# Weight low halves of the middle block by a negated copy and an adding transfer, the S5 recurrence on one engine, and a last section by token tiles

## What is computed

```
u = rms_norm(x, norm_pre);  p = u @ ev_w_in            # 1024 x 5120
a_in, a_z, b_val, b_gate, b_z = split(p)
ya = s5_layer(a_in, ...)        # s_t = Lbar s_{t-1} + Bbar u_t, 64 groups x 64 complex states
ya = gelu(ya); ya = ya * sigmoid(ya @ s5_w_glu + b_glu); ya = ya * silu(a_z)
h = b_val * sigmoid(b_gate)
h = causal depthwise conv of width 31 over the tokens
yb = (silu(layer_norm(h)) @ w_pw + b_pw) * silu(b_z)
x = x + rms_norm(concat([ya, yb]) @ ev_w_out, norm_post)
```

## Time and profile before

| | us |
|---|---|
| median of 3 runs (lowest, highest) | 1820.9 (1819.47, 1821.16) |
| the profiled execution, device time | 1818.73 |
| its span | 1817.0 |
| TensorE busy in the span | 1680.5 (92%) |
| VectorE busy | 1005.8 (55%) |
| ScalarE busy | 610.4 (34%) |
| GpSimd busy | 296.3 (16%) |
| mean granted TensorE clock, of full speed | 0.969 |

### The profile page before, as it was taken

The page is one execution under the profiler, slowest core; times in us unless marked ns, Lnnn a source line. Parts: engine busy times, 40 slices in busy tenths (PEclk is TensorE's granted clock), DMA queues, the critical chain, the costliest instruction groups (busy, mean ns, idle before and its releaser), DMA issues.

```text
span 1817.0 us, 20356 instructions
## 1 busy us (share of the span) xinstructions
PE 1680.5 (92%) x7876; PEld 1364.0 (75%) x7876; DVE 1005.8 (55%) x1271; ACT 610.4 (34%) x852; POOL 296.3 (16%) x316
## 2 busy tenths in 40 slices
PE   6999989999999999989977876999989999999995
PEld 5887878878888888879955656768877777787764
DVE  4375254552345244547999979965454344354434
ACT  4333322233212233343411214255245244243431
POOL 4980000000000000030199284200000000000000
PEclk9999999999999999999988898999999999999998
DMA  8556433233333322263312231115313122131211
GB/s 243 131 146 161 118 103 94 93 116 109 100 93 98 100 93 99 76 232 93 117 35 58 70 139 47 47 64 170 105 47 93 59 82 92 46 105 57 70 47 58
DMA packets 129467, 177.39 MB, mean 98 GB/s; under 512 B 50683, under 2 KB 61419, under 8 KB 128363
## 3 DMA queue, kind: packets, MB, share of 16 engines
q1 hardware_dynamic: 127563, 173.62, 30.9%
q10 hardware_dynamic: 1664, 2.13, 0.4%
q0 software_dynamic: 160, 0.52, 0.2%
HBM read 161.58 MB, written 14.68 MB: 97 GB/s over the span
## 4 chain that ended last, share of the span: by engine, by line
PE 76%; DVE 19%; ACT 2%; issue 1%; POOL 1%; SPq 0%; DMA 0%; ACTq 0%; DVEq 0%; POOLq 0%
PE PS L1960 67%; DVE TMP L1639 8%; DVE WL L1295 2%; PE PS L1938 2%; PE PS L2210 1%; PE PS L2228 1%; DVE FIX L1676 1%; DVE S L1678 1%; PE PS L2081 1%; PE PS L2219 1%; ACT XN L901 1%; DVE V L1373 1%; DVE SEGV L1610 1%; DVE S L1621 1%; DVE S L1618 1%
## 5 line engine op out<-in xcount | busy, mean ns | idle before, releaser
L1960 PE MATMUL PS<-HH,WH 128*128 128x512 f32 x1216 | 485.4, 399 | 46.5 <-DVE WL L1295 35.5
L1295 DVE TENSOR_TENSOR WL<-WR,WH 128x1024 fp32r<-128x1024 f32 x200 | 256.3, 1289 | 466.3 <-ACT WH L896 466.2
L1960 PE MATMUL PS<-HL,WH 128*128 128x512 f32 x1216 | 479.8, 395 | 0.0
L1960 PE MATMUL PS<-HH,WL 128*128 128x512 f32 x1216 | 479.3, 394 | 0.0
L896 ACT ACTIVATE WH<-WR 128x1024 fp32r<-128x1024 f32 x200 | 210.7, 1059 | 709.1 <-PE PS L1960 695.7
L1960 PEld LDWEIGHTS PS<-HH,WH 128*128 128x128 f32 x1216 | 232.6, 191 | 103.0 <-DVE WL L1295 30.7
L1960 PEld LDWEIGHTS PS<-HL,WH 128*128 128x128 f32 x1216 | 232.9, 192 | 49.1 <-issue 1.0
L1960 PEld LDWEIGHTS PS<-HH,WL 128*128 128x128 f32 x1216 | 232.3, 191 | 49.6
L1639 DVE SCALAR_TENSOR_TENSOR TMP<-CP,PRM,TMP 128x512 f32<-128x512 f32 x232 | 183.7, 838 | 0.0
L1960 PE MATMUL PS<-WH,HH 128*128 128x512 f32 x384 | 152.6, 397 | 6.5 <-DVE WL L1295 4.2
L1960 PE MATMUL PS<-WH,HL 128*128 128x512 f32 x384 | 151.6, 395 | 0.0
(11 more groups left out here) (312 smaller groups left out, 2039.3 us busy)
## 6 DMA issues: line engine op xcount, KB each, us to landing
WR<-in_w_in_dram SPq DMA_DIRECT2D x96, 512.0 KB, 3.7
WR<-in_ev_w_in_dram SPq DMA_DIRECT2D x40, 512.0 KB, 3.6
WR<-in_od_w_in_dram SPq DMA_DIRECT2D x32, 512.0 KB, 3.9
WR<-in_ev_w_out_dram SPq DMA_DIRECT2D x16, 512.0 KB, 3.6
WR<-in_od_w_in_dram SPq DMA_DIRECT2D x32, 256.0 KB, 3.3
WR<-in_od_w_out_dram SPq DMA_DIRECT2D x16, 512.0 KB, 3.8
WR<-in_w_branch_a_dram SPq DMA_DIRECT2D x8, 512.0 KB, 3.6
WR<-in_w_branch_b_dram SPq DMA_DIRECT2D x8, 512.0 KB, 3.6
```

The source lines that it names most:

```text
L1295: dve.tensor_tensor(WL[:, s, :, :], WR[:, s, :, :], WH[:, s, :, :].bitcast(F32), ALU.subtract).then_inc(w_lo, 1)
L1960: mm = pe.matmul(out_banks[m], st, mv, start=(kt == 0 and i == 0), stop=(kt == 2 * per - 1 and i == 2))
```

## The change

1. **Low halves.** For the chunks from a_in.0 to pw.1 (14 units, 56 chunks) VectorE no longer subtracts. ScalarE makes WH as before and right behind it WL = -W (L873 of the new kernel, semaphore w_neg). GpSimd then issues a transfer for each chunk that reads W from DRAM again and adds it onto WL in SBUF, whose landing counts w_summed of the slot; TensorE waits for w_summed instead of w_lo. As written, the low half comes out as the weight, rounded and negated, plus the weight. SP loads a chunk when w_neg says that the one four before is negated.
2. **Recurrence.** All 32 pairs on VectorE: 15 steps of five instructions of 512, 512, 512, 256 and 256 elements per partition, 7 carries of five short instructions, and 64 corrections of 420 elements. Fourteen steps and two instructions stand ahead of the gating of b_gate.1. GpSimd has none of it and does not gate YA either; VectorE does that.
3. **Order of taps.** 78 taps before the recurrence, 36 after it, 8 in the halves of y, 16 and 21 around glu, and the last 89 after everything that VectorE does for glu.
4. **Order of jobs.** TensorE runs glu, ev_a.0, mean, ev_a.1, var, pw. The centring reads the mean from PSUM.
5. **Last head.** Each token tile has both column halves made before the next; VectorE adds and weighs each half as it comes, ScalarE squares it; after a tile's second half one root, one reciprocal and one full-width operation follow.

```diff
@@ semaphores of the ring
+        w_neg, w_summed = sem("w_neg"), [sem(f"w_summed{i}") for i in range(RING)]
@@ SP
-                if n >= RING:
+                if summed(n - RING):
+                    sp.wait_ge(w_neg, n - RING - SUM_FROM + 1)
+                elif n >= RING:
                     sp.wait_ge(w_lo, n - RING + 1)
@@ GpSimd
+            def add_weights(job):
+                name, u = job.split(".")
+                for q in range(4):
+                    n = chunks_before(job) + q
+                    pool.wait_ge(w_neg, n - SUM_FROM + 1)
+                    pool.dma_start(WL[:, n % RING, :, :],
+                                   summands[name][q * 2 * P:(q + 1) * 2 * P, int(u) * NC:int(u) * NC + NC]
+                                   .rearrange("(k p) n -> p k n", p=P), accum_op=ALU.add).then_inc(w_summed[n % RING], 16)
@@ ScalarE
                     act.activation(WH[:, n % RING, :, :], WR[:, n % RING, :, :], ACT.Copy).then_inc(w_hi, 1)
+                    if summed(n):
+                        act.activation(WL[:, n % RING, :, :], WR[:, n % RING, :, :], ACT.Copy, scale=-1.0).then_inc(w_neg, 1)
...
             ya_halves(range(4, 8))
 
+            split()
+            act.wait_ge(h_lo, 32)
+            evac("ev_a.0", [YO[:, m, 0:NC] for m in range(4)], ACT.Copy)
             for kt in range(KT):
                 act.wait_ge(z_cent, kt + 1)
                 act.activation(SQ[:, kt, :], CP[:, kt, CPAD:], ACT.Square).then_inc(z_sq, 1)
             split()
-            act.wait_ge(h_lo, 32)
-            evac("ev_a.0", [YO[:, m, 0:NC] for m in range(4)], ACT.Copy)
+            evac("ev_a.1", [YO[:, m, NC:D] for m in range(4)], ACT.Copy)
             act.wait_ge(sq_used, KT)
             act.activation(RS[:, :], bank("var", 0), ACT.Sqrt, bias=EPS[:, 0:1]).then_inc(banks_act, 1)
@@ VectorE
-            split_convolve(24)
-            split_convolve(24)
-            convolve(44)
-            steps = step_ops()
-            split_convolve(20, steps)
-            split_convolve(12, steps)
+            convolve(78)
+            s5 = recurrence()
+            recur(s5, 42.0)
             times_tmp([("b_gate.1", m, CP[:, 4 + m, CPAD:]) for m in range(4)], GATEV)
             dve.wait_ge(tmp_free, 24)
-            split_convolve(20, steps)
-            split_convolve(24, steps)
-            for _ in steps:
+            for _ in s5:
                 pass
...
+            convolve(36)
...
                     convolve(1)
+                    dve.tensor_tensor(YA[:, kt, :], YA[:, kt, :], AZ[:, kt, :], ALU.mult).then_inc(ya_gated, 1)
...
-            split_convolve(24)
-            convolve(len(todo))
+            convolve(16)
             for u in range(2):
                 if u:
-                    split()
+                    convolve(21)
                     h_low(3, lambda kt: YA[:, kt, :], range(4))
                 dve.wait_ge(ya_gated, 4 * u + 4)
                 times_tmp([(f"glu.{u}", m, YA[:, 4 * u + m, :]) for m in range(4)], GLUV)
             h_low(3, lambda kt: YA[:, kt, :], range(4, 8))
+            convolve(len(todo))
@@ VectorE, the end
+            for t in range(TT):
+                last_add(t, 0)
+                if t == 0:
+                    dve.wait_ge(prow1_in, 16)
+                weigh(t, 0)
+                last_add(t, 1)
+                weigh(t, 1)
+                last_norm(t)
@@ TensorE
             section("glu", Y, ready(y_lo, 3))
+            section("ev_a", H, ready(h_lo, 3), rows=True, units=(0,))
             pe.wait_ge(ones_in, 1)
             pe.wait_ge(conv_done, 8)
...
-            section("ev_a", H, ready(h_lo, 3), rows=True, units=(0,))
+            section("ev_a", H, ready(h_lo, 3), rows=True, units=(1,))
             free("var")
...
-            section("ev_a", H, ready(h_lo, 3), rows=True, units=(1,))
             section("pw", Y, ready(y_lo, 4))
@@ TensorE, the last head
+                for t in range(1, TT):
+                    for u in range(2):
+                        for kt in range(4):
+                            step(t, u, kt)
```

More of the change, by code:

```diff
@@ L824, in _ @@
[L824 to L844, removed]
-                    tt(fix, by, end, ALU.mult)
-                    seq.wait()
-                    o = pool.tensor_tensor(into, into, fix, op)
-                    if q and n in (FIX_HALF - 1, len(FIX_POOL) - 1):
-                        o.then_inc(fixed_pool, 1)
-                        pool.wait_ge(fixed_pool, 1 + (n > FIX_HALF))
-                    else:
-                        seq.inc(o)
@@ L854, in _ @@
-            pool.wait_ge(banks_act, act_after("a_z2.1"))
-            for kt in range(KT):
-                pool.wait_ge(y_lo, 24 + kt + 1)
-                pool.tensor_tensor(YA[:, kt, :], YA[:, kt, :], AZ[:, kt, :], ALU.mult).then_inc(ya_gated, 1)
+            pool.tensor_scalar(LAM64[:, 2, :].unsqueeze(2), TAB[:, 1, :, SEG_CH - 1:SEG_CH], -1.0, None,
+                               ALU.mult, ALU.bypass).then_inc(powers, 1)
+            ev_in, ev_out = a["ev_w_in_2"][0], a["ev_w_out_2"][0]
+            summands = {"a_in": ev_in[:, EV_IN["a_in"]:], "b_val": ev_in[:, EV_IN["b_val"]:], "b_gate": ev_in[:, EV_IN["b_gate"]:],
+                        "a_z2": ev_in[:, EV_IN["a_z2"]:], "b_z2": ev_in[:, EV_IN["b_z2"]:], "glu": a["s5_w_glu_2"][0],
+                        "ev_a": ev_out[0:D, :], "pw": a["conv_w_pw_2"][0]}
@@ new lines, in recurrence @@
+                seq.wait(last)
+                dve.memset(BNA[:, 0, 0:1], 0.0).then_inc(carried, 1)
+                used = [last, last]
+                for b in range(FIX_BLOCKS):
+                    for q in range(2):
+                        made = []
+                        for ri in range(2):
+                            fix, into, by, end, op = correction(b, ri, q, ri)
+                            seq.wait(used[ri])
+                            made.append(seq.inc(dve.tensor_tensor(fix, by, end, ALU.mult)))
+                            yield 0.59
+                        for ri in range(2):
+                            fix, into, by, end, op = correction(b, ri, q, ri)
+                            seq.wait(made[ri])
+                            used[ri] = seq.inc(dve.tensor_tensor(into, into, fix, op))
+                            yield 0.59
+                    if b % 4 == 3:
+                        seq.wait(used[1])
+                        dve.memset(BNA[:, 0, 0:1], 0.0).then_inc(fixed, 1)
@@ L1880, in head @@
                 dve.wait_ge(y2_add, h * 8 + 8)
-                for u in range(2):
-                    if u and not last:
+                for u in range(0 if last else 2):
+                    if u:
                         hsplit(n, HEAD_CHUNKS + V_AT, 2)
@@ L2172, in _, with out_by_tile, step @@
             pe.wait_ge(banks_act, act_after("lr"))
+            def out_by_tile(n0, acts, kt_ready):
+                def step(t, u, kt):
+                    for i, (wi, ai) in enumerate(halves):
+                        mm = pe.matmul((B, A)[u][t], tile(acts(kt)[ai], t), (WH, WL)[wi][:, 2 * u + kt // 2, kt % 2, :],
+                                       start=(kt == 0 and i == 0), stop=(kt == 3 and i == 2))
+                    if kt == 3:
+                        mm.then_inc(halves_done, 1)
+                for kt in range(4):
+                    kt_ready(kt)
+                    for u in range(2):
+                        if kt % 2 == 0:
+                            pe.wait_ge(w_lo, n0 + (2 * u + kt // 2 + 1))
+                        step(0, u, kt)
+                for t in range(1, TT):
+                    for u in range(2):
+                        for kt in range(4):
+                            step(t, u, kt)
             def head(h, last):
```

209 lines of the change are left out of this document (102 added, 107 removed).

## The result

The changed kernel takes 1831.11 us in the median of 5 runs (1826.42 to 1831.21), the kernel before beside it 1820.64 (5 runs). The ratio is 1.0055, 95% interval 1.0043 to 1.0066: **10.5 us slower**, where no change was forecast (1820). The profiled execution took 1831.18, with a span of 1829.4, so 12.4 us over the 1817.0 of before. The executions of the changed kernel differ by 4.8 us among themselves.

What follows compares the result with a forecast made beforehand. TensorE, 92% busy, bounds the kernel, so only its idle stretches, where VectorE bounds, can pay. Middle +10.5 and end -11.1 give -0.6: 1818.73 becomes 1818.1, with 2.2 to the median 1820; range 1802 to 1848.

Steps and rivals of the forecast that it cites:

- Step 2: TensorE up to b_z2: waits for a_z2.1's first adding transfer, 962.6 to 967.0; 5.9 us with the restart.
- step 5: Last taps: VectorE idles about 30 us ahead of y, then makes 89 taps while TensorE stands 40 us before the mean.
- step 6: After var: pw.0 waits for loads, ScalarE's copies and the root, 31.9 us; ev_b.1 starts at 1320.2.
- step 7: Last head: product starts 1.4 us earlier, last VectorE work ends at 1802.8 instead of 1813.9, -11.1 us.
- Step 1: VectorE up to b_gate.1: a recurrence step takes 3.9 us, and the gating comes at 956.4.
- the +10.5 for the middle: From 897 to ev_b.1's start: ev_b.1 at 1320.2 instead of 1309.7, 10.5 us longer.
- the low bound, 2.9: Recurrence on VectorE: a step at the pace of contiguous elements takes 2.9 us, and the gate comes at 941.5.
- the likeliest case: Whole kernel as worked out in the timetable, range 1811 to 1829; chance 0.46.
- the outer one: Whole kernel: range 1802 to 1848, taking in the fast rival to its end and the rate-bound one.
- the faster one: Rival: recurrence at 2.9 us a step and pw.0's loads sooner by some 2 us; 1812, down to 1802; chance 0.26.
- The transfers' rate: Rival: load plus adding transfer take 6.2 us, over a chunk's 5.44, for some 32 chunks; +25, 1844; chance 0.14.
- VectorE against GpSimd: Rival: VectorE's taps hold up GpSimd's issuing of adding transfers; +15 (1834) if mild, else +34 and more; chance 0.14.

Runs made afterwards that it cites:

- experiment 1: Also taps_early: changed kernel with 92 instead of 36 taps between recurrence and y's halves, 33 instead of 89 behind glu; 1791.54 us, ratio 0.9846.
- experiment 2: Changed kernel with the loads of pw.0's four chunks issued ahead of SP's wait for var and X1; 1806.11 us, ratio 0.9926.
- experiment 3: Changed kernel with ten recurrence steps and two instructions ahead of the gating of b_gate.1 instead of fourteen and two; 1815.01 us, ratio 0.9974.
- experiment 8: Kernel before with the new last head alone; 1808.33 us, ratio 0.9934.
- experiment 6: Changed kernel with the 15 recurrence steps on elements side by side in eights instead of 16 apart, result not the reference's; 1815.5 us, ratio 0.9974.
- experiment 7: Changed kernel with GpSimd's 56 transfers copying W onto WL instead of adding it, low half wrong; 1825.74 us, ratio 1.0026.
- experiment 4: Changed kernel with the edits of experiment 1, experiment 2 and experiment 3 together; 1762.48 us, ratio 0.9687.

## Why the prediction failed, step by step

The times are those of the changed kernel's profiled execution against the timetable.

| step | forecast | measured | off by |
|---|---|---|---|
| recurrence starts | 899.4 | 903.1 | +3.7 |
| gate of b_gate.1 | 956.4 | 964.7 | +8.3 |
| a_z2.1 starts | 967.0 | 977.4 | +10.4 |
| b_z2.1 ends | 1033.7 | 1045.0 | +11.3 |
| glu.0 starts | 1069.9 | 1081.5 | +11.6 |
| glu.1 ends | 1114.8 | 1128.2 | +13.4 |
| mean starts | 1184.2 | 1197.0 | +12.8 |
| var ends | 1221.5 | 1234.4 | +12.9 |
| ev_b.1 starts | 1320.2 | 1334.1 | +13.9 |
| new end against old, from the last transposes | -11.1 | -11.4 | -0.3 |

**The mechanisms were right.** Step 2's gap (11.2 us, forecast 4.4), step 5's idle VectorE and block of taps, step 6's chain behind var (31.3 us, forecast 31.9) and step 7 are there, and experiments 1, 2, 3 and 8 show each by itself. The one gap of over a microsecond that the prediction doesn't speak of, 3.49 us ahead of ev_a.0, costs nothing, since the mean waits for the taps behind it. Step 5's idle time of VectorE was forecast at about 30 us and was 42.43: VectorE made up its delay behind the gate (64 corrections in 32.6 us instead of 38, and its 36 taps ended at 1033.5, forecast 1034), but y came as late as TensorE was. What failed are the sizes of four terms of the sum, in steps 1 and 2 and at the restarts, and with them the +10.5 for the middle, which measured 24.4.

**The terms that were mis-sized:**
- *Step 1, the step of the recurrence: 4.6 us.* 3.9 was carried from 128 and 64 elements; 512 took 1.05 instead of 0.97 and 256 took 0.63 instead of 0.56, so a step took 4.26. At the same stride the line through two narrow instructions ran 8 to 12% low, and there were 72 instructions in a row. Experiment 6 shows the stride to be the cause of the price; the low bound, 2.9, is the price of elements side by side (2.73 there).
- *Step 2, the addition: 2.1 us.* From WL's copy on ScalarE to TensorE's matmul it was taken at 6 and took 8.9, of which 8.5 in flight; ScalarE's side was 0.8 faster. The 6 was a load's 3.6 and, with no row for it, 2.4 for the second read and the issue together; experiment 7 shows 3.6 us in flight for the addition alone.
- *Restarts: 4.3 us.* The prediction had about 1.5 us for each, which is what glu.0 cost in the kernel before (1132.86). A restart at the lower level of the clock (0.43 us between matmuls, 0.23 at the upper) lasted six or seven matmuls there, and 10, 14 and 14 in the changed kernel, behind a_z2.1's gap, y and var: 0.9, 1.7 and 1.7 us more. The trace of before had such long ones too, 10, 12 and 14 matmuls behind its gaps at 929.89, 942.68 and 955.48; the prediction took the shortest of these four. A gap costs its own length and this.
- *Step 1, the queue ahead: 1.2 us.* Missed. ScalarE's second instruction per chunk also stands ahead of the evacuation of a_in.1: s5_t.1 waited for it 2.40 us instead of 1.45, and a_in went 0.2 slower. The prediction asked what is queued behind ScalarE's new instruction at the gate, and not here.
- *The start of the execution: 2.5 us*, which seems to be no effect of the change. By b_val.0's first matmul the changed kernel is 2.5 us late, in experiments 1 to 4, with the same program up to there, 0.5 to 1.3. The first 32 transposes are 1.4 of it: they took 6.49 us in this profiled execution against 5.11, with the same instructions. The rest came in short stretches further on.

They add up to 14.7, and small differences elsewhere take 0.8 back (0.6 of it between glu.1's end and the mean, 0.6 in the gap behind var), for the 13.9 in the table. Four terms of the sum were low, and none was high by more than this. They lie in series on one path, so they added, and the sum of +10.5 and -11.1 had no room for it: the range of the likeliest case, 1811 to 1829, missed by 2 us, the outer one to 1848 held. The outer range is where the rivals put it, and none of the three came about; the faster one needed a step of 2.9, and it took 4.26. *The transfers' rate* did not bind: 1.7 + 3.2 = 4.9 us of 16 engines for a chunk of 5.44, and an addition would have had to take 3.7. *VectorE against GpSimd* did not occur. (The 12.67 us on which it rests was the first of 15 operations of that line; their median in the kernel before is 1.27.) The line by which GpSimd issues, for the four weights:

```profile
L826 POOL DMA_DIRECT2D WL<-in_ev_w_in_dram x32: 1195/1204/1287, 821.2 to 1026.0; - x32
L826 POOL DMA_DIRECT2D WL<-in_s_w_glu_dram x8: 1204/1204/1204, 1031.0 to 1108.8; - x8
L826 POOL DMA_DIRECT2D WL<-in_ev_w_out_dram x8: 1204/1204/1222, 1114.8 to 1157.7; - x8
L826 POOL DMA_DIRECT2D WL<-in_conv_w_pw_dram x8: 1204/1204/1204, 1247.3 to 1293.0; - x8
```

All 56 take 1.2 to 1.29 us: the 21 that ran beside taps and those among the recurrence like the 16 during which VectorE did nothing. The taps lost nothing either; VectorE's timeline, first with seven issues beside it, then with one:

```profile
842.79 38.51 DVE L1654 SCALAR_TENSOR_TENSOR TMP<-CP,PRM,TMP 128x512 f32<-128x512 f32 x58
...
1157.10 38.50 DVE L1654 SCALAR_TENSOR_TENSOR TMP<-CP,PRM,TMP 128x512 f32<-128x512 f32 x58
```

The Trainium skill ("SBUF — State Buffer", section "Who interferes with whom") says that two-input VectorE instructions contend only with GpSimd's reads of SBUF, and with its inference that issuing needs the write interface the trace agrees.

Two readings of the prediction are loosely put and change no term: the 87.08 us behind var end at ev_b.1's first matmul, not its last tile (step 6 uses them rightly), and the mean's row names ScalarE's sigmoid of glu, which stood behind the last tap by way of VectorE's queue (that tap ended at 1181.78, the mean began at 1183.96).

## What to carry to other kernels

When an engine is relieved, look next at where its remaining work stands in its own queue: here it idled 42 us ahead of one wait and was waited for 42 us at the next, and moving 56 instructions across it was worth 38 us. When an order is changed so that a job no longer hides a wait (ev_a.1 over pw's loads and the root of var), follow what each queue holds back at that point, SP's above all: a load that needs nothing was standing behind a wait that it did not need. And when a forecast is the difference of two like terms, price every gap with the longest restart that the trace shows, not the shortest, and carry strided prices to wider instructions with a margin upwards (8 to 12% here).

## What the runs showed of the hardware that was not expected

- 512 elements per partition of a tensor_tensor whose one fp32 operand has its elements 16 apart take 1.05 us on VectorE, with the elements side by side in eights 0.69. With 256 elements, read and written in this way, it is 0.63 against 0.42.
- An adding transfer of 512 KB took 8.5 us in flight and 3.2 us of 16 engines, the same without the addition 4.9 and 1.7; issuing it took GpSimd 1.20 us, the plain one 0.71 (medians).
- Behind the second block's gaps of 4.5 us and more, ahead of matmuls of 128x512, TensorE ran at the lower clock for 6 to 14 of them before it was back at the upper one, and not for the same number each time: from pw.0's first matmul to ev_b.1's first took 67.3 to 68.5 us in the changed kernel and experiments 1 to 4, the same work each time. Executions of the changed kernel differ by 4.8 us, those of taps_early by 0.9; that these stretches are the reason was not tried.
